# Gate and up units of the second layer: order of the narrow and the wide product in a pair

## The reference, cut to what matters

```
FF_DIM = 2816
hn = rms_norm(x, norm_ffn_g[l])
gu = hn @ w_ffn_in[l]                                  # (256, 1024) @ (1024, 5632)
x  = x + (silu(gu[..., :FF_DIM]) * gu[..., FF_DIM:]) @ w_ffn_out[l]
```

## Time and profile before

| | |
|---|---|
| median of 3 runs | 826.19 us |
| the profiled execution's own time | 825.39 us |
| its span | 823.6 us |
| TensorE busy | 814.9 us, 99% of the span |
| granted TensorE clock, mean | 0.998 |
| memory reads | 186 GB/s over the span |

### The profile page before, as it was taken

The page is one execution under the profiler, slowest core; times in us unless marked ns, Lnnn a source line. Parts: engine busy times, 40 slices in busy tenths (PEclk is TensorE's granted clock), DMA queues, the critical chain, the costliest instruction groups (busy, mean ns, idle before and its releaser), DMA issues.

```text
span 823.6 us, 12737 instructions
## 1 busy us (share of the span) xinstructions
PE 814.9 (99%) x4962; PEld 719.0 (87%) x4962; DVE 612.4 (74%) x734; ACT 460.0 (56%) x628; POOL 152.8 (19%) x146
## 2 busy tenths in 40 slices
PE   8999999999999999999999999999999999999997
PEld 8999888888989999999999988778899888888885
DVE  6998888877786766565787898888687767565764
ACT  6757687534664454545564667855355554445544
POOL 2317754082000000000000385513300000000000
PEclk9999999999999999999999999999999999999999
DMA  9976445666545555645577565455644465645441
GB/s 297 298 231 203 161 160 191 210 202 226 167 154 185 181 195 190 218 154 203 161 221 234 167 217 176 158 204 176 213 158 168 154 205 175 223 163 203 155 177 52
DMA packets 103597, 156.17 MB, mean 190 GB/s; under 512 B 4080, under 2 KB 68898, under 8 KB 103552
## 3 DMA queue, kind: packets, MB, share of 16 engines
q1 hardware_dynamic: 102080, 153.50, 56.3%
q0 software_dynamic: 1296, 1.79, 0.8%
q10 hardware_dynamic: 176, 0.27, 0.1%
HBM read 152.39 MB, written 1.05 MB: 186 GB/s over the span
## 4 chain that ended last, share of the span: by engine, by line
PE 98%; DMA 1%; SPq 1%; DVE 0%; issue 0%; ACT 0%
PE bank L1090 20%; PE bank L1092 10%; PE bank L1035 8%; PE bank L978 8%; PE bank L1037 8%; PE bank L980 8%; PE bank L979 8%; PE bank L1036 8%; PE bank L1066 5%; PE bank L1067 5%; PE bank L1065 5%; DMA gates<-in_x 1%; PE bank L1175 1%; PE bank L1196 1%; PE bank L1024 0%; PE bank L1023 0%
## 5 line engine op out<-in xcount | busy, mean ns | idle before, releaser
L1442 DVE TENSOR_TENSOR w_lo<-raw,w_hi 128x2048 fp32r<-128x2048 f32 x135 | 318.9, 2363 | 132.3 <-ACT w_hi L648 131.6
L648 ACT ACTIVATE w_hi<-raw 128x2048 fp32r<-128x2048 f32 (+3 forms) x146 | 264.2, 1817 | 128.4 <-PE bank L1037 55.8
L1090 PE MATMUL bank<-act,w_hi 128*128 128x512 f32 x704 | 247.6, 395 | 0.0
L1092 PE MATMUL bank<-act,w_lo 128*128 128x256 f32 x704 | 197.0, 280 | 0.0
L1090 PEld LDWEIGHTS bank<-act,w_hi 128*128 128x128 f32 x704 | 132.0, 187 | 30.1
L1092 PEld LDWEIGHTS bank<-act,w_lo 128*128 128x128 f32 x704 | 132.9, 189 | 0.4
L1035 PE MATMUL bank<-w_hi,act 128*128 128x512 f32 x288 | 114.3, 397 | 0.0
L1037 PE MATMUL bank<-w_hi,act 128*128 128x512 f32 x288 | 112.3, 390 | 0.0
L1036 PE MATMUL bank<-w_lo,act 128*128 128x512 f32 x288 | 112.1, 389 | 0.0
L648 ACT ACTIVATE qk<-bank 128x256 f32<-128x256 f32 (+1 forms) x96 | 37.5, 394 | 75.9 <-PE bank L1092 75.8
L978 PE MATMUL bank<-act,w_hi 128*128 128x256 f32 x256 | 73.1, 286 | 1.0 <-DVE w_lo L1782 1.0
(11 more groups left out here) (250 smaller groups left out, 1451.1 us busy)
## 6 DMA issues: line engine op xcount, KB each, us to landing
raw<-in_w_ffn_in SPq DMA_DIRECT2D x44, 1024.0 KB, 5.1
raw<-in_w_gate SPq DMA_DIRECT2D x32, 1024.0 KB, 5.5
raw<-in_w_ffn_out SPq DMA_DIRECT2D x22, 1024.0 KB, 4.9
raw<-in_w_in SPq DMA_DIRECT2D x18, 1024.0 KB, 6.3
raw<-in_w_o SPq DMA_DIRECT2D x8, 1024.0 KB, 5.1
raw<-in_w_proj_b SPq DMA_DIRECT2D x4, 1024.0 KB, 4.9
raw<-in_w_in SPq DMA_DIRECT2D x12, 256.0 KB, 6.2
gates<-qk SPq DMA_DIRECT2D x32, 64.0 KB, 5.2
```

The source lines that it names most:

```text
L648: return nc.scalar.activation(o, i, ACT.Copy)
L1090: nc.tensor.matmul(bank[b + f], hi[:, k, fs], act2[:, k, :, :].rearrange("p h s -> p (h s)"), start=(k == 0), stop=False, skip_group_check ...
L1092: last = nc.tensor.matmul(main(b)[:, f, :], lo[:, k, fs], act_hi[:, k, :], start=False, stop=(k == KT - 1), skip_group_check=True)
L1442: V.tensor_tensor(w_lo[slot][:, :], raw[slot][:, :], w_hi[slot][:, :].bitcast(F32), ALU.subtract)\
```

## The change

A new function `ffn_half_narrow` does a whole half with the two products of each pair in the other order. The narrow product now opens the bank (`start`), and the wide product closes it (`stop`) and carries the signal of the half. `ffn_in` uses it in the last layer; the first layer keeps `ffn_half`. The gate and up unit that are written out by hand ahead of the loop keep `ffn_half` in both layers. That makes 10 steps of 2 units with 2 halves each, so 40 halves of 8 pairs.

```diff
+            def ffn_half_narrow(slot, b, f):
+                hi, lo, fs = kview(w_hi[slot]), kview(w_lo[slot]), slice(f * P, f * P + P)
+                for k in range(KT):
+                    nc.tensor.matmul(main(b)[:, f, :], lo[:, k, fs], act_hi[:, k, :], start=(k == 0), stop=False,
+                                     skip_group_check=True)
+                    last = nc.tensor.matmul(bank[b + f], hi[:, k, fs], act2[:, k, :, :].rearrange("p h s -> p (h s)"),
+                                            start=False, stop=(k == KT - 1), skip_group_check=True)
+                return last
...
             def ffn_in(l, slot, use, b, j):
                 weights(l, slot, use)
                 pe.wait_ge(bank_free[b], l * len(BANKS[b]) + (j + (FFN_FROM[b] + 1)))
-                ffn_half(slot, b, 0, range(KT)).then_inc(half_done, 1)
-                ffn_half(slot, b, 1, range(KT)).then_inc(w_used[slot], 1)
+                half = partial(ffn_half, ks=range(KT)) if l < L - 1 else ffn_half_narrow
+                half(slot, b, 0).then_inc(half_done, 1)
+                half(slot, b, 1).then_inc(w_used[slot], 1)
```

More of the change, by code:

```diff
@@ L22 @@
 from contextlib import ExitStack
+from functools import partial
 import numpy as np
```

## The result

| | median | runs | ratio to before |
|---|---|---|---|
| before | 825.67 us | 12 | |
| changed | 827.23 us (826.17 to 827.99) | 12 | 1.0016, 95% interval 1.0009 to 1.0023 |

So the change costs between 0.7 and 1.9 us. The prediction was 826.2 us, 824.0 to 827.8, with "no change", in the sense of less than 0.2%, as the likeliest case. The difference is clear of noise, since its interval begins above 1, and it is smaller than that 0.2%.

The account below looks back on a forecast made before the run. TensorE was taken as the bound, with no idle time: number of products by the distance between starts. All terms summed to 0, so the median stays at 826.2 us, range 824.0 to 827.8.

Parts of the forecast that it names:

- no change: Whole kernel: time within 0.2% (1.65 us), steps in any mix of two known forms, 824.9 to 827.0 us; chance 0.70.
- The pairs: Wide and narrow products in the ten steps: same products and loads, 353 or 347 ns a pair in both orders; difference 0.
- The seams: Where steps meet down units: the sequence of widths is the same, only shifted by one place; difference 0.
- ring of widths: Ten steps read as a cycle: 31 single wide products between narrow ones and one run of 25 wide, in both orders.
- The first product behind the transposes: First product after the 16 transposes, now narrow: start-up again 0.08 us; difference 0, bounds -0.08 and +0.08.
- The waits: TensorE's waits for low parts, bank and `ff_lo`: margins 1.7 to 7.3 us, so 0; at most 4.6 us without cover.
- who waits for a half: ScalarE's copy of the right half: signal still comes when all 16 products are done, so nothing behind it moves.
- Opening the bank: Narrow product with `start` in 40 halves: taken as 0, bounded at 0.08 us each, 3.3 us either way.
- the second one: Rival: ten steps settle slow, +0.8 us, 827.0; a third, slower form gives 828.9, chance 0.09.
- The signs of being wrong: Step windows outside 11.10 or 11.29 us, a half beginning with a longer distance, or the unchanged first layer's steps moving.

Follow-up runs that it names:

- the run with the same stationary operand: Changed kernel with the narrow product loading the high part of the weights, as the wide one does; stretch of the ten steps 163.29 us.
- the one with eight wide and eight narrow: Changed kernel with all eight wide products, then all eight narrow ones, in each half of the second layer's ten steps; stretch 162.05 us.
- narrow-first order with a break: Changed kernel with one single-column product put ahead of each gate unit of steps 1 to 10 of the second layer; stretch 164.1 us.

## Why the prediction was right, and where it was not

The case (no change beyond 0.2%) and the range held. The sum of 0 behind them did not: the stretch moved by +0.93 us, clear of noise, and the likeliest time, 826.2 us, lies 1.0 us under the median.

**The pairs: right.** Within a rhythm a pair costs the same in both orders: 353 ns in the slow one, before and after, and 347 ns in the quick one, in the quick steps of before and in the first step of after. The pairs are where most of the difference is paid, but only because more of them run in the slow rhythm, and that was the business of the next step.

**The seams: this step failed.** It read the two streams as the same ring of widths and took 0 for it. The ring is the same, but the distances depend on more than widths: also on whether a product reads an operand that begins off a multiple of 256 bytes. The run of 25 wide products holds both kinds, and the change puts them in another order. The term was 0 and measured +0.93 us: four quick steps turned slow, one slow step turned quick, and down units of 5.59 us, where the prediction wanted 5.56 to 5.58. The step had named the addresses that meet, and the place of the branch, as what is no longer the same, and gave them no price. The branch had no effect. The addresses that counted were not those of the pair's stationary operands (no effect either) but those of the down unit's operands. With the offset gone, the argument holds to 0.05 us.

**The first product behind the transposes: right.** Narrow, it took 0.20 us to the next start in the timeline of after (0.21 by the rounded starts), as its row had it:

```profile
645.04 0.36 PE L1091 MATMUL bank<-act,w_lo 128*128 128x256 f32 x1
645.25 0.40 PE L1093 MATMUL bank<-act,w_hi 128*128 128x512 f32 x1
```

**The waits and who waits for a half: right.** ScalarE's copies waited 37.2 us for TensorE over the end of the second layer (26 waits), against 36.7 before, and VectorE's subtraction 48.7 us for ScalarE in both. They held nothing up, as no product of the stretch has idle time before it. Lines of the waits from 644 us on before, and from 645 us on after:

```profile
DVE w_lo L1442 <- ACT w_hi L648: 48.7, 20, 2.5
ACT qk L648 <- PE bank L1092: 36.7, 26, 2.4
```
```profile
DVE w_lo L1454 <- ACT w_hi L649: 48.7, 20, 2.5
ACT qk L649 <- PE bank L1093: 37.2, 26, 2.5
```

**Opening the bank: right.** A narrow product with `start` costs nothing of its own; the quick first step, 11.19 us with its start-up, has four such openings, and without the start-up it is as long as a quick step before. (The bound in the prediction, 40 x 0.08, is 3.2 us and not 3.3.)

**The rivals.** What happened is the second one in its milder form, all steps but one in the slow rhythm; for all ten slow it had +0.8 us and 827.0. I had counted it in the case of no change, from 824.9 to 827.0, and the range reached to 827.8, which is why both held. (At 827.23 us the median is just above that case's own bound; the call held as a ratio, since the kernel before had 825.67 us in these runs and not 826.2.) That its price came so near has some luck in it: the four steps cost the 0.8 us, and the first step's -0.19, which it didn't have, was made up by +0.30 in the slow steps and down units, which it put at nothing. Its weight inside the case should have been larger: the alternation of before was itself a sign that equal steps can run in either rhythm, so that a change at a seam may redraw which of them are slow.

The formula that the prediction took from the Trainium skill (TensorE: Matmul & The Clock Gate, Back-to-back issue gap) stands there for isolated matmuls; for streams with a weight load for each, such as this one, the same section gives about 131 ns at 512 columns. The traces agree with neither: in none do two consecutive 512-column products start less than 223 ns apart. No term and no chance came from it.

**The signs of being wrong.** One of them was that the first layer's steps, which are not changed, move. Its second step did, by 0.06 us, with 0.07 us in the down unit behind it. As runs with the order of before show the same 11.30 us there, and one and the same program showed 11.30 and 11.10 us in two executions, this is scatter between executions and nothing shows it to be the change.

The rest of the difference between the medians (1.56 us, against 0.93 in the stretch) is not explained by a stage. The stretch alone would fit the interval of the ratio, which begins at 0.7 us, and where the stretch begins scatters: in the changed kernel, the run with the same stationary operand and the one with eight wide and eight narrow, which are one program up to there, it is 645.04, 644.71 and 644.25 us.

## What to carry to other kernels

Where matmuls follow each other without a gap, look at the distance of their starts step by step, not at a mean: if equal steps differ by a fixed amount, a change of order may deal the two lengths out anew, and a difference of 0.1% then need not come from the order itself. Long runs of one width and operands that begin on a multiple of 256 bytes gave the regular distances here, and together the only version that was faster than the kernel before by more than its interval. An alignment is worth testing in each place separately, since in the first layer the odd offset helped by 2.3 us.

## What the hardware showed that I had not expected

- The distance between products of one shape has several stable values at a clock of 1.00. Wide ones follow each other at 227 ns (5.44 us for 24) or at 232 to 233 ns (5.56 to 5.59 us), and a wide and narrow pair takes 347 or 353 ns. Behind the 232 ns is no even spacing: in the down unit at 672.30 us of the kernel before, single distances run through 228 to 241 ns and repeat, where the aligned ones settle at 226 to 227.
- In the second layer it repeats to the nanosecond scale: three kernels with the widths and offsets of before have a stretch of 162.37 us each, two with those of the changed kernel 163.29 us each. In the first layer the first three steps vary between such kernels (stretches of 162.37 to 162.73 us with the offset), and all are at 11.10 us from the fourth step on.
- Moving two small operands by 128 bytes changed the down units from 5.56 and 5.58 to 5.50 us (5.44 with long runs) in the second layer and from 5.69 to 5.76 us in the first, and the steps around them too.
- Open is what in the memory or the engine makes the offset count, and why a mixed stream settles in 347 or in 353 ns. Two steps in the narrow-first order with a break were quick and the third was not, and no run here tells why.
